# First mixer: latent projections ahead, values, gates and convolution products between attention steps; expert rows in pieces of 4 KB

## What is computed

```
proj = h @ w_in                      # 1,024 -> short conv b, c, h; GLA q, k, v, gate; low-rank gates; cq, ckv, kr; conformer a, gate
y_a = sc_b * depthwise_conv(sc_c * sc_h, w_sc_conv)             # 3 taps
y_b = rms_norm(gla_forward + gla_backward) * silu(gg)           # gated linear attention, both directions
y_c = blocked_attention(q_c, k_c, v_c)                          # 4 heads; q from cq, k and v from ckv, 32 roped dims
y_d = silu(layer_norm(depthwise_conv(a * sigmoid(gate), w_cfm_dw)))   # 31 taps
mix = concat(rms_norm(y_a), rms_norm(y_b), rms_norm(y_c), rms_norm(y_d)) @ w_out
h = layer_norm(alpha * h + mix); h = layer_norm(alpha * h + conv_ffn(h))
```

## Time and profile before

| | |
|---|---|
| runs | 3508.28 us median of 3 (3507.06 to 3511.01) |
| the profiled execution | 3503.07 us; span of its instructions 3501.4 us |
| mean granted TensorE clock | 0.915 |

### The profile page before, as it was taken

How to read it: one execution, slowest core, us unless ns; L and a number is a source line. 1 busy time by engine, 2 the same in 40 slices (tenths; PEclk the granted TensorE clock), 3 DMA queues, 4 the chain that set the end, 5 groups by cost and what they waited for, 6 DMA issues and landing times.

```text
span 3501.4 us, 44800 instructions
## 1 busy us (share of the span) xinstructions
PE 3024.2 (86%) x13284; PEld 2376.0 (68%) x13284; DVE 1873.9 (54%) x2709; ACT 1331.2 (38%) x1903; POOL 1196.9 (34%) x739
## 2 busy tenths in 40 slices
PE   5867799988868899979999995999399999959994
PEld 4745688866636688866777773887266777748873
DVE  3865444225854444035653315998547544258986
ACT  2124155313141455212134312888211344118883
POOL 2520444544303344533564350110144643511101
PEclk8987899998978899989899996999699999979996
DMA  4210233432101233522232243999322321339994
GB/s 126 64 37 3 76 96 97 137 120 76 56 13 37 84 96 96 169 73 66 64 97 61 61 132 120 389 398 399 114 80 61 94 69 54 101 141 358 398 398 160
DMA packets 406500, 461.46 MB, mean 132 GB/s; under 512 B 33396, under 2 KB 280262, under 8 KB 406280
## 3 DMA queue, kind: packets, MB, share of 16 engines
q1 hardware_dynamic: 386432, 392.05, 34.0%
q0 software_dynamic: 14976, 54.53, 4.1%
q10 hardware_dynamic: 4872, 12.26, 1.0%
HBM read 423.10 MB, written 35.65 MB: 131 GB/s over the span
## 4 chain that ended last, share of the span: by engine, by line
PE 45%; issue 21%; DVE 14%; POOL 8%; DMA 6%; ACT 4%; SPq 1%; POOLq 0%; DVEq 0%; ACTq 0%
PE bank L460 7%; PE bank L461 7%; POOL unit_lo L380 6%; DMA wt<-in_w 5%; DVE u L1240 4%; PE bank L1808 4%; PE bank L698 3%; PE bank L777 2%; PE bank L1942 2%; PE bank L1943 2%; PE bank L1946 2%; PE bank L778 1%; PE bank L780 1%; PE bank L1869 1%; PE bank L466 1%
## 5 line engine op out<-in xcount | busy, mean ns | idle before, releaser
L460 PE MATMUL bank<-xT_hi,unit_hi 128*128 128x512 f32 x1680 | 685.7, 408 | 19.4 <-DVE xT_lo L624 10.8
L461 PE MATMUL bank<-xT_lo,unit_hi 128*128 128x512 f32 x1680 | 665.2, 396 | 0.0
L364 POOL TENSOR_SCALAR unit_hi<-unit_raw 128x1024 fp32r<-128x1024 f32 (+2 forms) x248 | 248.0, 1000 | 1146.5 <-PE bank L698 373.3
L366 POOL TENSOR_TENSOR unit_lo<-unit_raw,unit_hi 128x1024 fp32r<-128x1024 f32 (+2 forms) x248 | 542.9, 2189 | 20.7
L380 POOL TENSOR_TENSOR unit_lo<-unit_raw,unit_hi 128x1024 fp32r<-128x1024 f32 x128 | 307.4, 2402 | 420.7 <-ACT unit_hi L374 420.7
L460 PEld LDWEIGHTS bank<-xT_hi,unit_hi 128*128 128x128 f32 x1680 | 322.6, 192 | 112.1 <-issue 37.4
L461 PEld LDWEIGHTS bank<-xT_lo,unit_hi 128*128 128x128 f32 x1680 | 322.4, 192 | 66.0 <-issue 1.9
L698 PE MATMUL bank<-xT_hi,unit_lo 128*128 128x512 f32 x1296 | 320.1, 389 | 0.0
L698 PEld LDWEIGHTS bank<-xT_hi,unit_lo 128*128 128x128 f32 x1296 | 243.2, 188 | 50.6
L374 ACT ACTIVATE unit_hi<-unit_raw 128x1024 fp32r<-128x1024 f32 x128 | 135.8, 1061 | 342.8 <-PE bank L698 172.6
L445 DVE TENSOR_TENSOR wt_lo<-wt,wt_hi 128x1024 fp32r<-128x1024 f32 x192 | 228.0, 1221 | 41.5 <-ACT wt_hi L440 41.1
(11 more groups left out here) (452 smaller groups left out, 6174.3 us busy)
## 6 DMA issues: line engine op xcount, KB each, us to landing
wt<-in_w SPq DMA_DIRECT2D x384, 512.0 KB, 10.8
unit_raw<-in_w_in SPq DMA_DIRECT2D x276, 256.0 KB, 3.1
unit_raw<-in_w_ffn_up SPq DMA_DIRECT2D x176, 256.0 KB, 3.2
unit_raw<-in_w_ffn_down SPq DMA_DIRECT2D x88, 256.0 KB, 3.1
unit_raw<-in_w_out SPq DMA_DIRECT2D x64, 256.0 KB, 2.8
y_rows<-yb POOLq DMA_DIRECT2D x32, 512.0 KB, 7.1
y_rows<-zeros POOLq DMA_DIRECT2D x24, 512.0 KB, 5.3
unit_raw<-in_w_br SPq DMA_DIRECT2D x96, 128.0 KB, 2.3
```

What stands on the lines that cost most here:

```text
L364: pool.eng.tensor_scalar(hi, raw, 1.0, 0.0, MUL, ADD).then_inc(self.hi_made, 1)
L366: pool.eng.tensor_tensor(lo, raw, hi.bitcast(F32), SUB).then_inc(self.split, 1)
L460: pe.matmul(out, wh, xh, start=first, stop=False)
L461: pe.matmul(out, wh, xl, start=False, stop=False)
```

## The change

Seven edits, all in the order and placing of work; the products are the same.

1. `ORDER` is now cq0, cq1, ckv, low-rank gates with kr, conformer a0 and gate0, then GLA q and k with the products of w_mla_uq and w_mla_ukv between them. These 8 chunks come before attention. The 4 units of values and gates and the other 8 chunks are cut into pieces (66 with two mean products) that PE takes, 3 or 4 at a time, between the score product and the value product of the attention steps (`FILL1`).
2. The GLA steps run in attention steps 6 to 14, with one PSUM bank for each kind of result instead of two (`B_SC` to `B_GO`); attention too has one bank for scores, one for transposes, one for outputs.
3. DVE does 8 taps before the ropes and the other 54 in steps 0 to 12 (`TAPS_AT`). The short convolution of one half comes in step 13, that of the other after the loop. Attention runs over query blocks outside and heads inside, so each block's output is divided in the loop (`attended`).
4. ACT makes hi for units 2 to 21 (`unit_done`) and also copies the transposed exponentials (pT) and the values, which DVE did. POOL makes only lo of these units.
5. Mean, norm and silu of the conformer, the two token-wise norms and the short convolution's norm now come at or after the end of the attention loop.
6. `rows_products` for w_out takes the units in `OUT_ORDER` = 2 to 7, 0, 1, waits for each pair of inputs on its own, and does the upper four banks of its first two units before the lower four.
7. For the experts' w1 and w3 partition p holds rows 8p to 8p + 7 of the matrix, two adjacent rows per unit, 4 KB in one piece; PE's transposes of xb take every eighth column.

```diff
+        ORDER = [13, 14, 15, 12, 0, 1, 10, 11, 2, 3, 6, 8, 4, 7, 9, 5]
+        U_UQ, U_UKV, U_GV, U_OUT, U_UP, U_DOWN = 6, 8, 10, 22, 30, 74
+        OUT_ORDER = (2, 3, 4, 5, 6, 7, 0, 1)
+        B_SC, B_TR, B_AV, B_GS, B_GKV, B_GO = 2, 3, 4, 5, 6, 7
+        KD_STEP, GLA_STEP = 5, 6
+        FILL1 = [4, 4, 4, 4, 3, 3] + [4, 4, 3] * 4
+        BEGUN = [("gv", j, 4) for j in range(4)] + [("chunk", k, 6) for k in range(8, 14)] + [("mean", 0, 1), ("chunk", 14, 6), ("var", 0, 1), ("chunk", 15, 6)]
+        TAPS0 = 8
+        TAPS_AT = [4, 2, 4, 4, 4, 5, 0, 0, 7, 6, 6, 6, 6]
...
+            def unit_done(j):
+                if j + SPLIT < U_OUT:
+                    ring.high(A, j + SPLIT, width=WIDTH1.get(j + SPLIT, 1024))
+                else:
+                    A.eng.wait_ge(ring.done, ring.products(A, j))
...
             for n in range(18):
                 if 0 < n < 17:
+                    if m >= 1:
+                        T.eng.wait_ge(at_te.sem, at_te.at(T, m))
...
+                if n < 16:
+                    pe.matmul(bank[B_SC][:], qh[0:MD, hh, i * P:i * P + P], kh[0:MD, hh, :], start=True, stop=True).then_inc(at_s.sem, at_s.up(T))
+                for _ in range(FILL1[n]):
+                    next(dense)
                 if n > 1:
...
+                if n == KD_STEP:
+                    gla_keys()
+                if GLA_STEP < n <= GLA_STEP + 8:
+                    gla_output(n - GLA_STEP - 1)
+                if GLA_STEP <= n < GLA_STEP + 8:
+                    gla_scores(n - GLA_STEP)
...
+            rows_products(T, U_OUT, KC, xT_hi, xT_lo, late=banks_free, order=OUT_ORDER, ready=rows_ready)
...
-                    src = t[("w1_2", "w3_2")[w]][bass.ds(l, 1), e, :, :].rearrange("o (k p) n -> (o p) k n", p=P)[:, 2 * k:2 * k + 2, :]
+                    src = t[("w1_2", "w3_2")[w]][bass.ds(l, 1), e, :, :].rearrange("o (p k) n -> (o p) k n", p=P)[:, 2 * k:2 * k + 2, :]
...
+                src = src[:].rearrange("p (c k) -> p k c", k=KC)
...
-                        last = pe.transpose(bank[y][:, k * P:k * P + P], src[:, (4 * y + k) * P:(4 * y + k + 1) * P], ident)
+                        last = pe.transpose(bank[y][:, k * P:k * P + P], src[:, 4 * y + k, :], ident)
```

More of the change, by code:

```diff
@@ L753, in rows_unit @@
                 dst = ring.raw[(first + k) % RAW]
-                ring.load(E, first + k, [(dst[:, x:x + S], w[:, k, x:x + S]) for x in (0, S)])
+                row = order[k] if order else k
+                ring.load(E, first + k, [(dst[:, x:x + S], w[:, row, x:x + S]) for x in (0, S)])
         def splits1(G):
             for j in range(U_UP + SPLIT):
-                ring.part(G, j, width=768 if j == U_UQ else 512 if j == U_UKV else 1024)
+                if SPLIT <= j < U_OUT:
+                    ring.low(G, j, width=WIDTH1.get(j, 1024))
+                else:
+                    ring.part(G, j)
             with G.eng.Fori(0, FC // 2) as i:
@@ new lines, in whole, with dense_work @@
+            def whole(k):
+                for _ in projected(k):
+                    pass
+            def dense_work():
+                for what, k, _ in BEGUN:
+                    if what == "gv":
+                        yield from values(k)
+                    elif what == "chunk":
+                        yield from projected(k)
+                    elif what == "mean":
+                        T.eng.wait_ge(proj_ev.sem, proj_ev.at(T, 13))
+                        T.eng.wait_ge(c_done.sem, c_done.at(T, 1))
+                        for i in range(2):
+                            last = pe.matmul(bank[1][:], mean_of[:], u[:, i, :], start=i == 0, stop=i == 1)
+                        last.then_inc(cfm_mm.sem, cfm_mm.up(T))
+                        yield
+                    else:
+                        T.eng.wait_ge(rms_in.sem, rms_in.at(T, 1))
+                        rms_t(T, 2, 3, 2, 1)
+                        yield
@@ new lines, in scalar1, with begun_by, beside @@
+            evicted(7)
+            A.eng.wait_ge(head_rope.sem, head_rope.at(A, 5))
+            for hh in range(1, MH):
+                act.activation(kh[R0:MD, hh, :], kh[R0:MD, 0, :], ACT.Copy).then_inc(k_cp.sem, k_cp.up(A))
+            def begun_by(pieces):
+                at, k = 0, 0
+                while k < len(BEGUN) and at + BEGUN[k][2] <= pieces:
+                    at, k = at + BEGUN[k][2], k + 1
+                return k
+            def beside(n):
+                if n == 0:
@@ new lines, in scalar1 @@
+            rstd_a(A, 2, 1)
+            for what, k, _ in BEGUN[ended:]:
+                if what == "chunk":
+                    evicted(k)
+            load_gb(A, t["ln1_g"][bass.ds(l, 1), :], t["ln1_b"][bass.ds(l, 1), :])
+            for i in range(2):
+                A.eng.wait_ge(cfm_ln.sem, cfm_ln.at(A, i + 1))
+                act.activation(u[:, i, :], u[:, i, :], ACT.Silu, bias=col(B_CF + i)).then_inc(a_step.sem, a_step.up(A))
+            A.eng.wait_ge(a_step.sem, a_step.last(A))
@@ L1390, in vector1 @@
+            for i in range(2):
+                v.tensor_tensor(ya[i], ya[i], rstd[:, 0, :], MUL).then_inc(y_val.sem, y_val.up(V))
+                V.eng.wait_ge(y_val.sem, y_val.last(V))
+            gain_v(V, 0, 6, [u[:, i, :] for i in range(2)])
+            gain_v(V, 2, 0, ya)
             norm_v(V, 0, U_OUT + KC - 1)
```

797 lines of the change are left out of this document (415 added, 382 removed).

## The result

| | before | after |
|---|---|---|
| median of the runs | 3509.65 us (4 runs, 3507.06 to 3512.45) | 3396.99 us (4 runs, 3393.37 to 3403.86) |
| the profiled execution's span | 3501.4 us | 3391.6 us |
| mean granted clock | 0.915 | 0.928 |

The ratio is 0.9684 with a 95% interval of 0.9672 to 0.9695: 111 us faster, where 84 were forecast.

A forecast was written before the change was run, and what follows sets the result against it. No single engine bounds the kernel: DVE, dependent chains and attention in the mixers, PE then DMA in the experts. 3503.1 - 75 (both mixers) - 9.5 (experts) = 3418.6, plus 5.2 from profiled execution to median: 3424 us; range 3398 to 3475.

The forecast's parts named there:

- Maxima 8 and 13 at 135 and 189 us: Mixer's attention steps: DVE's score maxima of steps 8 and 13, timed from the first projection product.
- Steps level between PE and DVE: The mixer's 18 attention steps: PE's own work 125 us, DVE's 133 us, so the later one counts in each step.
- Dense products keep the clock up: Attention steps: argument against the slow-clock case (chance 0.08, 3555 us); dense products in every step, as where the clock was 0.90.
- Row order: w_out: starts at 241 us in the walk; ya's lo half, ready at 251, isn't missed because rows 0 and 1 come last.
- Experts: Experts' w1 and w3 in 4 KB pieces: DMA's loss goes, results stored every 17.7 us, 9.5 us less for both layers.
- strided reads: Rival in the experts: PE's transposes of every eighth column cost double, 27.8 us over 32 experts, total 3452; chance 0.13.
- pieces not joined: Rival in the experts: DMA doesn't join the rows into 4 KB, everything else as forecast, total 3433; chance 0.07.
- the 10 us (4%) for hand-overs: Each mixer: added to the walk for waits between engines, moving w_out's start from 241 to 251 us.
- The walk: Mixer: instruction-by-instruction timing from the first projection product through attention to w_out, which starts at 241 us.
- hand-overs eat half: Rival in the attention steps: engines wait for each other twice a step with single banks, 18 us per mixer, 3462; chance 0.17.
- POOL's disturbance of DVE: Attention steps: POOL's lo halves slow DVE's taps by 2.0 us per unit, 14 units, 28 us of DVE's work.
- w_out at 46.9 us: Each mixer's output product: still takes 46.9 us, starting at the slow clock as before.

The follow-up runs named there:

- DVE's gap in step 8 closed: Changed kernel with divisions of blocks 1 and 2 one step earlier, and 4 of step 8's 7 taps ahead of its GLA read: 3386.06 us, ratio 0.9638.
- The early division: Changed kernel, but DVE divides the attention output of blocks 1 and 2 one step earlier, in steps 9 and 13: 3384.7 us, ratio 0.9646.
- lo halves small: Changed kernel, but POOL writes only 8 of 1024 columns of the lo halves of units 2 to 21: 3379.05 us, ratio 0.9624.
- four such edits: On the changed kernel: early division, 3384.7 us; taps ahead of GLA reads, 3395.7; with early division, step 8's taps ahead, 3386.06, or fifth swap earlier, 3380.09.

## Why the prediction was right, and where it was off

**Right, and shown.** *First score product after 72 us*: 72.6. *Maxima 8 and 13 at 135 and 189 us*: 134.4 and 191.4. *PE's end of the steps at 215*: 219.0. *Steps level between PE and DVE*: with the dense work taken out DVE's steps 10 and 11 stay as they are, and with DVE's gap in step 8 closed PE's next steps stay as they are. *Dense products keep the clock up*: 0.90 to 0.96 over stretches of the steps, and 0.69 when they are taken out; single steps behind a wait fell with them too (0.77 in step 10). *Row order*: 8 us in the trace. *Experts*: 9.2 us of 9.5 with their edit alone, and both rivals there (strided reads, pieces not joined) refuted; the packets of the page fell from 406,500 to 373,732.

**Right in part by luck: maximum 13.** The prediction gives steps 8 to 12 9.7 us each, 48.5 in all, yet puts 54 between its maxima 8 and 13 without naming the other 5.5. The trace has 57.0, in steps of 13.5, 9.9, 14.8, 8.3 and 10.4 us. The total is near, the steps are not the five equal ones of the forecast.

**Mis-sized: the 10 us (4%) for hand-overs.** The walk by itself said 241 us, the trace 243.4, so the added term was hardly there: w_out came 7.6 and 8.3 us ahead of the 251, 16 of the 27 us by which the forecast was too high. That the durations and the gaps between starts that the walk was made of already held the hand-overs is the likely reason; no run tests it. The reason that the prediction gave for the term, 21% "issue" in the chain, was a misreading (see the result): the share is 20% after the change too.

**Missed: the wait for the single output bank.** From maximum 8 to maximum 15 the walk had 65 us, the trace 71.2. The early division takes 6.1 us out of the steps (6.0 of them behind maximum 8) and up to 6.9 out of the mixer, so in sum the difference is this wait, with the half clock behind it. DVE's gap in step 8 (3.7 us) isn't in the walk either, but closing it gave nothing. The prediction's rival "hand-overs eat half" named single banks; it was there, at one place, at somewhat over a third of its 18 us per mixer. Behind the steps the walk erred the other way: from maximum 15 to w_out it had 41 us, the trace 37.8, so its 241 is nearer to 243.4 than its parts were.

**Mis-sized: POOL's disturbance of DVE.** The sum had 14 units of 2.0 us, 28 us of DVE's work, in the steps. Only 10 units fall between the first maximum and the last. From the one to the other DVE is busy 96.1 us, and 83.6 with their lo halves small: 12.5 us, 1.3 a unit. The steps get 6.6 us shorter. The mistake did little harm: the walk used 1.2 us per step in steps 8 to 12 (6 us; the small lo halves give 3.9 there), and PE's own work stood right behind. With lo small PE is busy 114.5 of the 121.2 us. The stretch from the first to the last maximum, in the changed kernel and with lo small:

```profile
125.73:253.51 127.78, 116.40 (x557) 89.32 (x556) 96.09 (x145) 43.21 (x80) 24.84 (x10) 0.95 0.14 42
```

```profile
122.15:243.34 121.19, 114.46 (x559) 88.60 (x558) 83.55 (x145) 43.43 (x80) 2.73 (x10) 0.97 0.15 44
```

**Mis-sized: w_out at 46.9 us.** In the forecast it still started at the slow clock; it starts at the full clock from its second product on and takes 1.6 us less, 3 us in both mixers. The prediction hadn't looked at what runs just ahead of w_out: mean products and transposes.

**Not forecast, and not shown to be the change's.** 4.3 us in the second block's unchanged code and 1.2 us more than 9.5 in the experts; both lie within what the same code differs by from profile to profile. Together: 16.6 in the two mixers, 3.3 in w_out, 4.3 and 1.2, about the 25 us between the forecast's sum of 3418.6 and the profiled execution's 3393.4.

## What to carry to other kernels

When latent or narrow steps wait on each other, look for dense work that depends on neither and cut it into pieces between them; its price is the pieces times PE's duration only in those steps where PE is the longer engine, and elsewhere what its weight units cost the other engine. When durations and start-to-start gaps come from a trace, be slow to add a share for hand-overs on top (here it was 7.6 us per mixer too much), and look instead for each buffer that lost its double, and on whose queue its release stands. A wait closed on one engine is worth what the other engine's own work and its clock leave free: one of four such edits here gave 12 us, the others nothing that the runs can tell from none.

## What the runs showed of the hardware

- PE reading fp32 at every eighth word for transposes: 275 ns against 272.
- Experts' weights in pieces of 4 KB: 411 to 415 GB/s in windows of 7 us, 411 over 209 us; w1 and w3 in pieces of 2 KB, 389.
- PE after 7.7 us of idle time started w_out at the half clock (47.3 us); after 5 us of mean products and transposes it ran w_out's second product at the full clock (45.0 us).
- POOL's two-operand instruction of 2.4 us stretches one of DVE's instructions on SBUF by about 2 us (a tap of 0.76 us to 2.78), but a maximum over a PSUM bank beside it took its usual 0.69 us. POOL, and DVE in the changed kernel:

```profile
130.27 2.40 POOL L382 TENSOR_TENSOR unit_lo<-unit_raw,unit_hi 128x1024 fp32r<-128x1024 f32 x1 [12.78 <-ACT unit_hi L375]
```

```profile
130.44 0.69 DVE L1470 TENSOR_REDUCE mmx<-bank 128x1 f32<-128x512 f32 x1 [0.80 <-PE bank L1026]
```

So what a unit costs depends on what DVE does in those 2.4 us, which the flat 2.0 us per unit didn't allow for. This is one such pair; how far it accounts for the 1.3 us a unit isn't worked out.
